# One barrier a stage, and first operands that cross the passages between stages, in a two-layer hybrid decoder kernel

## The reference

```python
# layer 0
h = rmsnorm(x, g0);  p = h @ w_in                    # columns split among two attentions
a = dilated_mixture_attention(q, k, v)               # 8 heads of 64, three (window, dilation) branches
b = causal latent attention, 8 heads                 # low-rank q and kv, keys of 64 + 32 rotary
x = x + concat(a, b) @ w_out
x = x + hierarchical_moe(rmsnorm(x, g_moe0))
# layer 1
x = x + mamba2_ssd_mixer(rmsnorm(x, g1))             # in-projection, conv, chunked scan, gated norm, out-projection
x = x + hierarchical_moe(rmsnorm(x, g_moe1))
return rmsnorm(x, g_final)
# hierarchical_moe: 4 groups of 8 experts; per token the best group, the 2 best experts in it;
# each expert: (silu(h Wg) * (h Wu)) Wd with inner width 512
```

## Time and profile before

| | |
|---|---|
| three runs | 2833.12, 2836.54, 2842.06 us; median 2836.54 us |
| the profiled execution | 2830.54 us, its span 2828.7 us, mean granted PE clock 0.97 |
| busy in it | PE 2652.8 us (94%), DVE 1882.6 (67%), ACT 1604.9 (57%), POOL 544.4 (19%) |
| DMA | 618.70 MB, 219 GB/s as a mean |

### The profile page before, as it was taken

One profiled execution on the slowest core, in us unless ns is written; L12 is line 12 of the kernel. 1 busy time (PEld: TensorE's weight loads), 2 busy tenths in 40 slices (PEclk: granted clock), 3 DMA queues, 4 the chain that ended last, 5 costly groups with the idle time before them and its releaser, 6 DMA issues. The chain is left out here.

```text
span 2828.7 us, 40392 instructions
## 1 busy us (share of the span) xinstructions
PE 2652.8 (94%) x13859; PEld 2140.8 (76%) x13859; DVE 1882.6 (67%) x2208; ACT 1604.9 (57%) x2027; POOL 544.4 (19%) x462
## 2 busy tenths in 40 slices
PE   8998999987999999987999999998997999999992
PEld 7886667775888888876788887787884788888881
DVE  6335766535888888876572542885534888888885
ACT  4234555323888888865331233882111888888882
POOL 0000000001444444420000000440000344444440
PEclk9999999998999999998999999999998999999996
DMA  4215110024999999966242324983104899999994
GB/s 172 79 45 172 39 46 24 30 82 175 378 380 379 384 387 382 382 255 208 71 121 76 114 86 163 325 262 122 45 23 165 330 390 382 373 381 381 378 369 193
DMA packets 237958, 618.70 MB, mean 219 GB/s; under 512 B 31928, under 2 KB 76496, under 8 KB 237712
## 3 DMA queue, kind: packets, MB, share of 16 engines
q1 hardware_dynamic: 206704, 558.35, 54.6%
q0 software_dynamic: 19136, 33.61, 3.2%
q10 hardware_dynamic: 12000, 25.17, 2.6%
HBM read 566.55 MB, written 86.13 MB: 231 GB/s over the span
## 5 line engine op out<-in xcount | busy, mean ns | idle before, releaser
L2627 DVE TENSOR_TENSOR moe_w_low<-moes_raw,moe_w_high 128x2048 fp32r<-128x2048 f32 x384 | 864.9, 2286 | 146.3 <-ACT moe_w_high L2556 146.2
L2556 ACT ACTIVATE moe_w_high<-moes_raw 128x2048 fp32r<-128x2048 f32 x384 | 721.4, 1915 | 71.7 <-PEq L150 56.7
L2420 POOL COPY moe_pick<-moes_tokens 128x1 int32 (+1 forms) x64 | 107.0, 1672 | 579.6 <-PE moe_px L2469 578.5
L174 PE MATMUL moe_py<-moe_w_high,moe_h_high 128*128 128x512 f32 x512 | 209.2, 409 | 0.0
L174 PE MATMUL moe_pg<-moe_w_high,moe_x_high 128*128 128x512 f32 x512 | 204.3, 399 | 0.0
L174 PE MATMUL moe_pu<-moe_w_high,moe_x_high 128*128 128x512 f32 x512 | 204.2, 399 | 0.0
L176 PE MATMUL moe_py<-moe_w_high,moe_h_low 128*128 128x512 f32 x512 | 200.7, 392 | 0.0
L176 PE MATMUL moe_pg<-moe_w_high,moe_x_low 128*128 128x512 f32 x512 | 200.4, 391 | 0.0
L176 PE MATMUL moe_pu<-moe_w_high,moe_x_low 128*128 128x512 f32 x512 | 200.4, 391 | 0.0
L175 PE MATMUL moe_py<-moe_w_low,moe_h_high 128*128 128x512 f32 x512 | 200.1, 391 | 0.0
L175 PE MATMUL moe_pu<-moe_w_low,moe_x_high 128*128 128x512 f32 x512 | 199.6, 390 | 0.0
(11 more groups left out here) (420 smaller groups left out, 6132.4 us busy)
## 6 DMA issues: line engine op xcount, KB each, us to landing
moes_raw<-in_w_gate SPq DMA_DIRECT2D x128, 1024.0 KB, 8.2
moes_raw<-in_w_up SPq DMA_DIRECT2D x128, 1024.0 KB
moes_raw<-in_w_down SPq DMA_DIRECT2D x128, 1024.0 KB, 8.6
sproj_raw<-in_w_in_ssd SPq DMA_DIRECT2D x28, 512.0 KB, 4.3
XC<-pre SPq DMA_DIRECT2D x24, 512.0 KB, 5.1
HN<-plan_hn SPq DMA_DIRECT2D x16, 512.0 KB, 3.2
pre<-Y SPq DMA_DIRECT2D x16, 512.0 KB, 7.1
Z<-sproj_z SPq DMA_DIRECT2D x32, 256.0 KB, 2.4
```

What stands on the lines that cost most here:

```text
L174: nc.tensor.matmul(out, lh, rh, start=start, stop=False)
L2420: nc.gpsimd.tensor_copy(pick[a][:, :], M.tokens[:, bass.ds(b, 1)]).then_inc(picked[a], 1)
L2556: nc.scalar.activation(wh[c % SPLIT_SLOTS][:, :], M.raw[j][:, :], ACT.Copy).then_inc(w_high, 1)
L2627: nc.vector.tensor_tensor(wl[j][:, :], M.raw[c % RAW_SLOTS][:, :], bits(wh[j][:, :]), ALU.subtract).then_inc(w_low, 1)
```

## The change

- `Stage.__exit__` no longer clears and has no second barrier: it hands its semaphores to a list, which POOL clears alone at the start of a later block, while the other engines work. The list is cleared once more at the end of the program. The 16 increments of the experts' stage are issued by SP in the router's stage, and its extra barrier is gone.
- mla to att: 512 columns of the first pair's Q and K are loaded in mla (`K.first`, in the new shared buffer `gain`). The 34 transposes of `keep_busy` at attention's start are gone. SP no longer waits in mla for its stores to land; it does so in att before it loads the latent heads' operands.
- out and sout: 1/rms of tiles 0 to 6 and the normed rows of tiles 0 and 1 (`hn_first`, which lie where the attention masks were) are made before the last addition into X, with the gain loaded there. In out a dummy Sqrt, for its table, comes first on ACT.
- router: the logits' eight matmuls go alternately to PE's columns 0 and 64 of the array (output partitions 0 to 35 and 64 to 99); the turn back multiplies by a matrix that adds both parts. The first gathers and the list of experts past the first 32 are moved to the start of the experts' stage.
- end of experts: SP waits for the scatters and loads tile 0's rows of Y (and in layer 1 the final gain) before the exit barrier. sproj loads its first weight piece ahead of tile 1's rows.
- sout: the gate's gain is multiplied into the weights as they are split, not into the rows.
- closing stage: four output buffers, and the last tile in two halves.

```diff
 class Stage:
...
-    def primed_block(self):
-        for s in self.loop_sems:
-            self.nc.sync.sem_inc(s, PRIMED)
-        self.nc.all_engine_barrier()
+    def block(self, clear=True):
+
+        if clear and Stage.spent:
+            self.nc.clear_and_free_semaphores(Stage.spent)
+            Stage.spent = []
         return self.ctx.enter_context(self.nc.Block())
 
     def __exit__(self, kind, *rest):
         self.ctx.close()
         if kind is None:
-            self.nc.clear_and_free_semaphores(self.sems)
-            self.nc.all_engine_barrier()
+            Stage.spent = Stage.spent + self.sems
...
 def mla_stage(nc, K, A, F):
...
+            for n, src in enumerate((K.QA, K.KA)):
+                sp.dma_start(K.first[n], src[0:2, :, 0:HALF].rearrange("a r n -> (a r) n")).then_inc(K.first_in, 16)
...
-            sp.wait_ge(kr_stored, 16 * HB)
-            for a in range(2):
-                sp.wait_ge(k_stored[a], 16 * NT)
-                sp.wait_ge(q_stored[a], 16 * (NT // 2))
...
+                if p == 0 and t < EARLY:
+                    return K.first[0][rows, :], K.first[1][rows, :]
...
-            keep_busy(nc, K, tp[0][:, 0, :], 34)
...
+            nc.scalar.activation(spare[:, :], K.ones[:, 0:1], ACT.Sqrt)
             high(0)
...
+                if t == NT - 2:
+                    dve.wait_ge(squares, NT - 1)
+                    V.tensor_scalar(K.rstd[:, 0:NT - 1], K.ssq[:, 0:NT - 1], 1.0 / D, EPS, ALU.mult, ALU.add).then_inc(mean, 1)
+                    dve.wait_ge(root, 1)
+                    V.reciprocal(K.rstd[:, 0:NT - 1], K.rstd[:, 0:NT - 1]).then_inc(rstd_ok, 1)
...
-            rows_of(0)
-            for n in range(RAW):
+            load(0)
+            rows_of(1)
+            for n in range(1, RAW):
                 load(n)
-            rows_of(1)
...
-                nc.scalar.activation(yh[n % 2][:, :, :], whole[n % 2][:, :, :], ACT.Copy).then_inc(high_ok, 1)
+                nc.scalar.activation(yh[n % 2][:, :, :], tp[n % 2][:, :, :], ACT.Copy).then_inc(high_ok, 1)
...
-                V.tensor_tensor(whole[n % 2][:, :, :], tp[n % 2][:, :, :], g, ALU.mult).then_inc(kept, 1)
...
-                    last = nc.tensor.matmul(lg[j % 2][0:NL, 0:CH], wr[:, k, :], hT[j % 2][:, k, :], start=(k == 0), stop=(k == ND - 1))
+                    first = k % 2 * P // 2
+                    last = nc.tensor.matmul(lg[j % 2][first:first + NL, 0:CH], wr[:, k, :], hT[j % 2][:, k, :], start=(k < 2), stop=(k >= ND - 2))
...
+                for first in (0, P // 2):
+                    last = nc.scalar.activation(lt[first:first + NL, j * CH:(j + 1) * CH], lg[j % 2][first:first + NL, 0:CH], ACT.Copy)
...
+            for a in range(2):
+                sp.wait_ge(stored[a], n * 16 + 32)
+            for k in range(2):
+                sp.dma_start(K.y_rows[k], Y[k * S:k * S + P, :]).then_inc(K.y_in[k], 16)
...
-    RING = 4
+    RING, OUT = 4, 4
...
+            return [slice(0, D)] if t < NT - 1 else [slice(0, HALF), slice(HALF, D)]
```

More of the change, by code:

```diff
@@ L766, in attention_stage @@
         ov = [st.ps(f"ov{b}", [P, 4, P]) for b in range(2)]
[L767 removed]
+        loaded = [st.sem(f"loaded{a}") for a in range(2)]
         scored, masked, exped, t_lo, t_hi, lo_kept, hi_kept, recip, summed, spread_ok, out_ok = (st.sem(n) for n in (
@@ L1021, in _ @@
                 square(t - 1)
+            act.wait_ge(mean, 1)
+            nc.scalar.activation(K.rstd[:, 0:NT - 1], K.rstd[:, 0:NT - 1], ACT.Sqrt).then_inc(root, 1)
             square(NT - 1)
@@ L1050, in sb @@
             return ctx.enter_context(nc.sbuf_tensor(name, shape, F32))
+        K.first, K.first_in = [K.gain[:, n * HALF:(n + 1) * HALF] for n in range(2)], outer.sem("first_in")
+        K.kr_stored = outer.sem("shared_stored")
+        K.q_stored, K.k_stored = ([outer.sem(f"{n}_stored{a}") for a in range(2)] for n in "qk")
         with ExitStack() as early:
@@ L1112, in ssd_project_stage @@
     with Stage(nc, "sproj") as st:
-        raw = [st.sb(f"raw{j}", [P, D]) for j in range(RAW - 1)] + [K.pre[:, 4 * S + 2 * (LEFT + S):5 * S + 2 * (LEFT + S)]]
+        raw = [K.gain[:, :], st.sb("raw1", [P, D]), K.pre[:, 4 * S + 2 * (LEFT + S):5 * S + 2 * (LEFT + S)]]
         with ExitStack() as early:
@@ L1929, in weights @@
                 for k in range(first, last):
-                    nc.scalar.activation(wh[:, k, :], w[:, k, :], ACT.Copy).then_inc(w_high, 1)
+                    g = V_GATE + half * NK + k
+                    nc.scalar.activation(wh[:, k, :], w[:, k, :], ACT.Copy, scale=K.vecs[:, g:g + 1]).then_inc(w_high, 1)
             weights(0, 0, EARLY)
@@ L1944, in _ @@
             square(ITEMS - 2)
+            act.wait_ge(mean, 2)
+            nc.scalar.activation(K.rstd[:, 0:NT - 1], K.rstd[:, 0:NT - 1], ACT.Sqrt).then_inc(root, 1)
             square(ITEMS - 1)
@@ L2168, in turn_back @@
                 for t in (2 * j, 2 * j + 1):
-                    last = nc.tensor.transpose(plogits[:, t, :], lt[:, t * P:(t + 1) * P], K.ident[0:NL, 0:NL])
+                    last = nc.tensor.matmul(plogits[:, t, :], lt[:, t * P:(t + 1) * P], fold[:, :], start=True, stop=True)
                 last.then_inc(logits, 1)
@@ L2413, in _ @@
                 load(n, c, e[BLOCK_OF[c]])
+            if layer:
+                sp.dma_start(K.gain[:, :], A["final_norm"].partition_broadcast(P)).then_inc(K.final_in, 16)
+            for a in range(2):
+                sp.wait_ge(stored[a], n * 16 + 32)
+            for k in range(2):
+                sp.dma_start(K.y_rows[k], Y[k * S:k * S + P, :]).then_inc(K.y_in[k], 16)
         @block.gpsimd
@@ L2802, in _ @@
             if final is not None:
-                for a in range(2):
-                    act.wait_ge(stored[a], 16 * (NT // 2))
+                for a in range(OUT):
+                    act.wait_ge(stored[a], 16 * (NT // OUT + (a == OUT - 1)))
                 act.nop()
```

283 lines of the change are left out of this document (169 added, 114 removed).

## The result

The changed kernel takes 2785.5 us as the median of four runs (2784.2 to 2786.88), against 2837.57 (2833.12 to 2842.06) for the kernel before beside it: 52.1 us less, a ratio of 0.9822 with a 95% interval of 0.9808 to 0.9836. The forecast was 2780, the range 2764 to 2798.

What follows compares the result with a forecast made beforehand. The prediction took PE, busy 94% of the span, as the bound, with gains in the passages between stages. Their sum, -56.0 us, took 2830.54 to 2774.5; with 6.0 from profiled execution to median, 2780 us, range 2764 to 2798.

Steps and rivals of the forecast that it cites:

- out to plan0 and sout to plan1: Passages into the two routers: tiles ready early and logits in two column groups, -12.0 us each, -24.0 together.
- The rival that logits don't overlap: Routers: the two column groups don't run side by side, 14.4 us not gained, 2793 us; chance 0.12.
- Attention's passage: mla to att: scores start 10.9 us earlier, less table load and half clock, -7.7 us in sum.
- the clock's 2.7 us: Attention's first steps run at half clock without the warm-up; charged 2.7 us, between 0 and 8.
- The other side, rounds that lose pace: Experts' rounds: weights arrive out of order and all 32 rounds pay; 2.0 us a round gives 2844; chance 0.03.
- plan to experts: Router to first expert product, twice: gathers issued after the barrier, transposes at once on landing; -2.9 us each, -5.8 together.
- so I charge 1 us: Start of the experts' stage: allowance of 1 us for the gathers running beside DVE's splitting.
- moe1 to closing: Experts to closing stage: first addition -6.75 us, no store waits -4.9, last tile's store -0.2, tile 1 0.8 late; -11.0.
- moe0 to sproj: Experts to sproj: tile 0's rows loaded early, so the norm's multiply on ACT and PE's first product come earlier; -2.6 us.
- scan to sout: Scan to sout: barriers -0.6, DVE's multiply gone -2.1, half-clock stretch after PE's wait avoided -1.7; -4.4 us.
- The barrier's price: Stage ends: second barrier with its clearing costs about 0.6 to 0.7 us, an outer stage's 0.4 more.
- I expect the same here: Whole kernel: the median lies 6.0 us above the profiled execution, as before, taking 2774.5 to 2780 us.

Runs made afterwards that it cites:

- e1: The changed kernel with all eight matmuls of a logits group sent to the same PE columns; 2797.6 us, 0.9875 of the kernel before.
- e6: The changed kernel with 18 warm-up transposes at the end of mla and 22 at the end of sproj, ahead of the barrier; 2785.0 us, ratio 0.9826.
- e3: The changed kernel, but DVE's first weight split in the experts' stage waits until POOL has issued both gathers; 2776.7 us, 0.9797 of the kernel before.
- e2: The changed kernel, but SP starts the experts' weight stream only when both first gathers have landed; 2780.1 us, 0.9814 of the kernel before.
- e9: The changed kernel with the first two gathers issued in the router's stage again, ahead of the exit; 2780.5 us, 0.9812 of the kernel before.
- e0: The changed kernel again, unchanged, for a second trace; 2785.1 us, 0.9831 of the kernel before.
- e4: The changed kernel with the weight stream held for both gathers' landing and DVE's first split for both issues; 2780.9 us, 0.9804 of the kernel before.
- e5: The changed kernel with the 34 warm-up transposes back at attention's start; 2787.5 us, 0.9840 of the kernel before.
- e11: The changed kernel with weights and split held, 18 transposes ending mla, out's dummy Sqrt behind its weight splits, last tile whole; 2774.5 us, 0.9788 of before.
- e10: The changed kernel with two output buffers again in the closing stage and the last tile whole; 2790.6 us, 0.9843 of the kernel before.
- e7: The changed kernel with a second barrier again at the end of each of 16 stages, without clearing; 2789.9 us, 0.9830 of the kernel before.

## Why the prediction was right, and where it was not

**Right, by its steps.** The passages out to plan0 and sout to plan1 came to -12.1 and -12.0 against -12.0, and e1 shows the columns' part in it, 5.9 to 6.2 for each; the rest goes by the argument of the forecast (rows made early, missing loads), which no run tests. The rival that logits don't overlap fell; the rate of attention's two column groups carried over to 36 columns. Attention's passage: -8.5 against -7.7, with the clock's 2.7 us confirmed by e6 (2.55). That 2.7 matched as a sum; it lay between 0 and 8 and rested on a guess of how long the half clock would last. The dummy Sqrt cost 0.9 as forecast. The other side, rounds that lose pace, didn't come: moe0 and moe1 took 569.3 and 569.9 us against 570.2 and 570.0.

**Wrong in size.** "plan to experts" was to give -2.9 each from the point where "the tokens are there"; it gave -0.3 and +0.5, and the -1.9 of the table is the clock in the router's last product. The steps that failed are "so I charge 1 us" for gathers beside DVE's splitting and the flight of "about 4 us". The second gather was to be down 9.8 us after the tokens and was so after 12.9: its issue was 1.9 us longer (e3), and its flight 6.0 us when a weight load was issued into it, against 3.3 without (e2). The sum had left this out by taking the flight from the earlier trace rows. e9 shows that the move by itself lost 4.9 us. "moe1 to closing" gave -10.1 instead of -11.0: the first addition waited for tile 0's rows, which SP had issued 3.5 us ahead of the exit, and the last store took 0.9 longer, not 0.2 less. In six other traces (e0, e2, e4, e5, e6, e11) the first addition came 8.8 us after moe1, not 9.6, which is the -6.7 forecast for it. "moe0 to sproj" gave -2.0 instead of -2.6; which of its landings was late was not tested. "scan to sout" gave -2.2 instead of -4.4: the half-clock stretch of 3.4 us wasn't avoided but came 100 us later, in the stage's second half, 1 us after a wait of 1.8 us. e1, e9 and e10 had this wait without the stretch. In e1, e5, e6, e7, e9, e10 and e11 the stage took 190.2 to 191.6 instead of 192.9, so that term holds in some executions. And the second trace of the kernel before had its stretch 27 us into the stage, not behind the wait ahead of it, so the step from that wait to the stretch isn't shown. The barrier's price was right for barrier and clearing together, and e7 shows that a barrier alone is half of it.

**The level.** The passages sum to -49.3 in the traces, 6.7 us short of the forecast's -56.0, of which the experts' passages are 3.9 (6.0 without the clock in the router's last product) and sout's clock 1.7. The medians differ by 52.1 us here and by 47.7 between e0 and the kernel before beside it; -49.3 lies between, and what is left is the spread of single runs. Luck has a part in how near the total came: 2.1 us of it are the clock in the router's last product, which no step of the forecast had named. The step from the profiled execution to the median, "I expect the same here", doesn't hold as a rule: the kernel before was profiled 6.0 us below the median that I started from, the changed one 1.4 above its own, since unchanged stages ran 5.7 us longer in that trace.

## What to carry to other kernels

A software gather that is moved out of a stage in which DVE is idle into one in which DVE works and a weight stream starts can lose more than the barrier it leaves: hold the DVE operation until it is issued (here this held the weight load too). Where a matmul's stationary operand is narrow, alternating its contraction between two column groups nearly halves it, and on a critical chain that can be the largest term. Before a stage's length is compared between two traces, its granted clock is to be compared: code that is the same here differed by 5 us.

## What the runs showed of the hardware

- A POOL drain outlasted the scatters: with SP past its wait for the last of them before 2744.69, it ended at about 2748.0, 6.7 us after its start. In e9, behind two gathers, it lasted 5.6 us and ended 3.4 after the last issue, about the 3.3 of flight in e2, so there no outlasting is shown.
- PE's granted clock fell only some time after an idle time: in attention 2.4 us into the next work. It came up after 5.9 us of nothing but transposes in the kernel before, and in e6, with 18 transposes in the gap, it didn't fall, against what the Trainium skill says of transposes ("TensorE: Matmul & The Clock Gate", Part 4: PE-mode transpose). A half-clock stretch came early in the scan in every trace that I compared, 3.4 to 13.7 us long and at different places, and the stage took 167.3 to 172.9 us.
- A DVE `tensor_tensor` of 2.28 us stretched a software gather's issue on POOL from 1.00 to 2.94 us, and a 1 MB weight load issued into the gather's flight went with 6.0 us of it instead of 3.3.
- A barrier of all engines cost 0.33 us on the path (e7), the clearing of a stage's semaphores about as much.
